# Delta stage: decayed keys and decayed state by scaled ACT copies in place of GpSimd products

## The reference, cut to what matters

```python
kd = k * jnp.exp(gc[..., -1:] - gc)[..., None]      # keys times the remaining decay
gl = jnp.exp(gc[..., -1])                           # decay over the whole chunk
def step(state, inp):
    u_n, w_n, qk_n, qg_n, kd_n, gl_n = inp
    v_new = u_n - jnp.einsum('bhtd,bhdv->bhtv', w_n, state)
    o = jnp.einsum('bhtd,bhdv->bhtv', qg_n, state) + jnp.einsum('bhts,bhsv->bhtv', qk_n, v_new)
    state = state * gl_n[..., None, None] + jnp.einsum('bhsd,bhsv->bhdv', kd_n, v_new)
    return state, o
```

## Time and profile before

| | us |
|---|---|
| median of 3 runs | 3032.19 |
| lowest, highest | 3027.72, 3032.43 |
| the profiled execution, its own time | 3031.88 |
| its span in the profile | 3029.9 |

### The profile page before, as it was taken

How to read it: one execution, slowest core, us unless ns; L and a number is a source line. 1 busy time by engine, 2 the same in 40 slices (tenths; PEclk the granted TensorE clock), 3 DMA queues, 4 the chain that set the end, 5 groups by cost and what they waited for, 6 DMA issues and landing times. The chain is left out here.

```text
span 3029.9 us, 42610 instructions
## 1 busy us (share of the span) xinstructions
PE 2863.9 (95%) x17750; PEld 2342.2 (77%) x17750; DVE 1450.3 (48%) x2014; ACT 1177.7 (39%) x1861; POOL 1001.0 (33%) x540
## 2 busy tenths in 40 slices
PE   6988998999999989989989999999889999999999
PEld 4788977878888757889768788887577767788887
DVE  4565556437616345655573375262584552441120
ACT  3563645323313235627552332221443652342232
POOL 2263021014534422630210244443442223344433
PEclk9999999999999999999999999999998999999999
DMA  5101202333423241022023333231522223333332
GB/s 161 34 28 60 80 1 71 94 101 91 116 79 103 58 112 54 5 69 70 2 71 104 104 91 111 82 103 45 122 77 60 70 61 87 86 97 98 92 89 77
DMA packets 419840, 235.92 MB, mean 78 GB/s; under 512 B 24020, under 2 KB 416706, under 8 KB 419010
## 3 DMA queue, kind: packets, MB, share of 16 engines
q1 hardware_dynamic: 419650, 233.20, 27.2%
HBM read 226.88 MB, written 6.29 MB: 77 GB/s over the span
## 5 line engine op out<-in xcount | busy, mean ns | idle before, releaser
L2066 POOL TENSOR_TENSOR WLO<-RAW,WHI 128x1024 fp32r<-128x1024 f32 (+1 forms) x205 | 534.3, 2611 | 982.7 <-ACT WHI L1947 982.7
L144 PE MATMUL PS<-HHI,WHI 128*128 128x512 f32 x2016 | 798.7, 396 | 24.7 <-POOL HLO L563 14.6
L145 PE MATMUL PS<-HLO,WHI 128*128 128x512 f32 x2016 | 790.5, 392 | 0.0
L146 PE MATMUL PS<-HHI,WLO 128*128 128x512 f32 x2016 | 790.4, 392 | 0.0
L144 PEld LDWEIGHTS PS<-HHI,WHI 128*128 128x128 f32 x2016 | 381.1, 189 | 118.1 <-POOL HLO L563 16.2
L145 PEld LDWEIGHTS PS<-HLO,WHI 128*128 128x128 f32 x2016 | 381.0, 189 | 83.1 <-issue 2.7
L146 PEld LDWEIGHTS PS<-HHI,WLO 128*128 128x128 f32 x2016 | 380.6, 189 | 82.5
L1947 ACT CAST WHI<-RAW 128x1024 fp32r<-128x1024 f32 (+1 forms) x208 | 227.4, 1099 | 550.0 <-PE PS L146 538.2
L2060 DVE TENSOR_TENSOR X<-X,PS 128x512 f32<-128x512 f32 x48 | 33.0, 688 | 372.4 <-PE PS L146 372.4
L144 PE MATMUL PS<-MHI,WHI 128*128 128x512 f32 x384 | 153.7, 400 | 16.0 <-DVE WLO L2019 11.1
L2043 DVE SCALAR_TENSOR_TENSOR ACC<-GP,PARS,ACC 128x512 f32<-128x512 f32 x88 | 162.8, 1850 | 3.1
(11 more groups left out here) (456 smaller groups left out, 5110.8 us busy)
## 6 DMA issues: line engine op xcount, KB each, us to landing
RAW<-in_w_up SPq DMA_DIRECT2D x88, 512.0 KB, 3.8
RAW<-in_w_in SPq DMA_DIRECT2D x82, 512.0 KB, 4.0
RAW<-in_w_mlp SPq DMA_DIRECT2D x64, 512.0 KB, 4.1
RAW<-in_w_down SPq DMA_DIRECT2D x32, 704.0 KB, 4.6
RAW<-in_w_in SPq DMA_DIRECT2D x20, 1024.0 KB, 5.4
RAW<-in_w_gate SPq DMA_DIRECT2D x32, 512.0 KB, 4.0
RAW<-in_w_out SPq DMA_DIRECT2D x24, 512.0 KB, 4.3
x_kept<-X SPq DMA_DIRECT2D x2, 2048.0 KB, 9.0
```

The lines of the kernel that those rows point to most:

```text
L144: e.matmul(out, wh, xh, start=first and n == 0, stop=False)
L145: e.matmul(out, wh, xl, start=False, stop=False)
L146: last = e.matmul(out, wl, xh, start=False, stop=final and n == len(quads) - 1)
L2066: pool.tensor_tensor(slot(WLO, u), source(u), slot(WHI, u), ALU.subtract).then_inc(lo_s, 1)
```

## The change

GpSimd's two functions go. ACT gets functions of the same names: for each lane four `activation(..., ACT.Copy, scale=...)`, one a head, whose scale is the column of LD or EL of that head, with the same semaphores at the end (`kd`, `sd`) and the same waits in front (`st` or `ld`, and `su`). In ACT's order, the keys of lane 0 stand ahead of `keep(2)`, those of lane 1 ahead of `keep(3)`, and the state of both lanes behind `keep(5)`.

```diff
@@ GpSimd
-                def keys_decayed(m, d):
-                    pool.wait_ge(S["st"][d], m) if m else pool.wait_ge(S["ld"][d], 2)
-                    c = chunk(m, d)
-                    pool.tensor_tensor(B[d]["KD"], tok(KTOK, c), wide(B[d]["LD"][:, c, :], P), ALU.mult).then_inc(S["kd"][d], 1)
-
-                def state_decayed(m, d):
-                    pool.wait_ge(S["su"][d], m)
-                    pool.tensor_tensor(B[d]["SD"], B[d]["ST"][:, :, :], wide(B[d]["EL"][:, chunk(m, d), :], P), ALU.mult).then_inc(S["sd"][d], 1)
...
                             level_mask(m, d, 5)
-                        if m and j < CH - 1:
-                            keys_decayed(j, d)
-                            if j:
-                                state_decayed(j, d)
@@ ACT
+                def keys_decayed(m, d):
+                    if m < CH - 1:
+                        if m:
+                            act.wait_ge(S["st"][d], m)
+                        else:
+                            act.wait_ge(S["ld"][d], 2)
+                        c = chunk(m, d)
+                        for h in H4:
+                            last = act.activation(B[d]["KD"][:, h, :], tok(KTOK, c)[:, h, :], ACT.Copy, scale=B[d]["LD"][:, c, h:h + 1])
+                        last.then_inc(S["kd"][d], 1)
+
+                def state_decayed(m, d):
+                    if 0 < m < CH - 1:
+                        act.wait_ge(S["su"][d], m)
+                        for h in H4:
+                            last = act.activation(B[d]["SD"][:, h, :], B[d]["ST"][:, h, :], ACT.Copy, scale=B[d]["EL"][:, chunk(m, d), h:h + 1])
+                        last.then_inc(S["sd"][d], 1)
...
                         for d in lanes:
                             keep_last(j, d)
+                        keys_decayed(j, 0)
                     keep(2)
                     if after:
                         for d in lanes:
                             grown(m + 1, d)
                         decays(m + 1, 0)
+                    if m:
+                        keys_decayed(j, 1)
                     keep(3)
...
                     keep(5)
+                    if m:
+                        for d in lanes:
+                            state_decayed(j, d)
                     if after:
                         for d in lanes:
                             corner_times_beta(m + 1, d)
```

## The result

| | before | after |
|---|---|---|
| median of 9 runs each, us | 3029.61 | 3044.95 |
| lowest, highest | 3026.85, 3039.07 | 3042.04, 3047.78 |
| the profiled execution, its own time | 3031.88 | 3043.67 |
| its span | 3029.9 | 3041.6 |
| mean granted clock of TensorE | 0.977 | 0.975 |

The ratio is 1.0048, 95% interval 1.0037 to 1.0058. By this ratio it is 14.5 us more (the two medians lie 15.3 us apart), slower beyond what the scatter explains. The forecast was 3036.5 us with a range of 3031.5 to 3040.5 and "same" as its likeliest side. It was wrong.

The account below looks back on a forecast made before the run. TensorE, busy 95% of the span, was taken to bound the kernel by its own order. Delays of 1.19 + 0.99 = 2.18 us a layer, 4.36 in two, on 3032.19 gave 3036.5 us, range 3031.5 to 3040.5.

Parts of the forecast that it names:

- The price of a group: Four added ACT copies of 128x128 in the delta stage take 1.19 us, between 1.01 and 1.56 us.
- The direct delay: Lane 1's keys ahead of keep(3) make TensorE's level_d 3 late by 1.19 us in m = 1, 0.99 in m = 2.
- Rival A: TensorE has more slack, or ACT's freed order absorbs the groups: no change, 3032 us; chance 0.11.
- The hidden groups: Lane 0's keys, lane 1's in m = 3 and the state copies fall in ACT's waits and cost nothing.
- GpSimd's relief: Twenty products leaving GpSimd free 20.7 us of its time, worth nothing on the path.
- Rival D: GpSimd's relief counts, removing three 0.59 us gaps a layer: 3033 us with the delay, 3028.7 without; chance 0.05.
- Rival C: The added ACT copies don't overlap, a group taking 1.56 us: 3038.0 us; chance 0.09.
- No fall of the clock behind the new gaps: TensorE's clock stays at 1.00 behind the gaps ahead of level_d 3, 1.47 us in m = 1, about 1.0 in m = 2.
- Rival B: TensorE's clock falls behind the new gaps, 1.26 us a fall: 3039.0 us for two, 3041.6 for four; chance 0.07.
- the sum: Delays of 1.19 and 0.99 us make 2.18 us a layer, 4.36 us in two, added to the time of before.
- So it moves along, and the next stage starts behind the last product: A late level_d 3 in the delta stage isn't given back; everything behind it shifts by the same delay.
- if the time moved by more outside these two stages: Sign of being wrong: time changing by more outside the two delta stages, one a layer, that the change touches.

Follow-up runs that it names:

- keys1_behind: Kernel after, with the keys of lane 1 moved behind keep(3) and the gates of lane 1 in ACT's order; 3030.85 us, ratio 1.0009 to before.
- idle_copies: Kernel before, GpSimd's products kept, plus four unread ACT copies ahead of keep(3) in m = 1 and 2 of both layers; 3042.49 us, ratio 1.0042.
- filled pair: Kernels after and before plus unread TensorE products in the idle times of hgrn_stage; 3030.1 us (0.9985) and 3029.84 us (0.9983).
- low_on_vector pair: Kernels before and after with the FL subtraction of hgrn_stage moved from GpSimd to VectorE; 3017.11 us (0.9950) and 3018.55 us (0.9955).

## Why the prediction was wrong, point by point

- **The price of a group: right.** 1.19 us forecast, 1.17 measured. By the formula that was quoted from the Trainium skill (ScalarE: Activation LUTs, What ACT_TABLE_LOAD costs) 1.17 was the estimate; the trace agrees with it.
- **The direct delay: right in place, a little too large.** Forecast gaps of 1.47 and about 1.0 us, measured 1.30 and 0.76 to 0.77. The forecast let L868 start where L881 had; it starts 0.11 to 0.13 us sooner behind the second EG copy (in m = 1 187.91 - 187.42 = 0.49 us behind that copy's start, where L881 had 188.84 - 188.22 = 0.62), which takes that much off both gaps; why it does was not tried. 3.6 us in place of 4.36, and the stages grew by 2.4 and 1.8 for a forecast of 2.2 each. Rival A, no change, falls by the gaps.
- **The hidden groups: right.** keep(2) has 0.42 us to spare (0.4 forecast); in m = 3 1.60 us is left; the state's copies and the copies to O hold up nothing. keys1_behind shows it in the time: 1.0009 with these groups in place.
- **GpSimd's relief is worth nothing: right, as far as the times tell** (keys1_behind, idle_copies). Rival D falls: the 0.59 us gaps are still there. Rival C, copies that don't overlap, falls by the 1.17 us.
- **No fall of the clock behind the new gaps: right,** at 1.30, 0.77 and (idle_copies) 1.45 us. Rival B had the right mechanism and the wrong place: it priced a fall only at the gap that the change makes, and at 1.26 us, where one in `hgrn_stage` cost about 1.6. That its sum for four falls, 3041.6 us, lies nearest to the measured time is luck.
- **The step that failed is the sum:** "So it moves along, and the next stage starts behind the last product", and then 4.36 us added to the time of before. That holds only if every later stage takes as long when it starts 2 us later; the term for the later stages stood at nothing, without a reason. It was not weighed, though the earlier trace rows showed the low clock in this kernel and though the prediction itself named "if the time moved by more outside these two stages" as a sign of being wrong. What the runs showed in its place: hgrn 2, which the change doesn't touch, is 4.6 us longer by three falls of the clock, and the 14.5 us come down to 0.3 when the idle times of `hgrn_stage` are filled and to 1.4 when they are shortened. In its level work TensorE waits seven times for VectorE's operands, up to 2.3 us at a time; in the profiled before, three falls lay in it in layer 1 and none in layer 2, at the same idle times. Whether the clock falls behind such a wait isn't set by the wait alone. A delay upstream goes with it: none in layer 2 in three traces without a delay, two or three in each of seven traces with one.

How much of 14.5 us this is: the base plays no part, since the 14.5 are a difference (the three runs of before that the forecast stood on had a median of 3032.19, the nine 3029.61). 3.6 us is the direct delay. Three falls in hgrn 2 are some 4.8 us. In layer 1 the four traces with a delay ahead in that layer have 2 or 3 falls and the six without have 0 (twice), 2 or 3 (four times), so anything from nothing to 4.8 us more in a median, which single traces can't pin down. The filled pair shows by the time itself that 14.2 of the 14.5 us go when these idle times are filled, and the low_on_vector pair that 13 go when they are shortened, in each case with part of the direct delay made up in other stages. These shares overlap, and no run separates them to the microsecond; that the idle times of `hgrn_stage` carry most of what goes beyond the 3.6 us is shown by those two pairs, and that they act through falls of the clock by the level-work table; the exact split is not shown.

What stays open: why a later start brings the falls in layer 2 each time, when the idle times ahead of them look the same, whether delays of other sizes than those run here (1.5 to 3.5 us in one layer, 3.6 in two) would bring them or take them away, and why the median of before itself moves between sets from 3027.0 to 3034.2 us: each set ran on another chip, and the median of the granted clock went with it (0.978, 0.976, 0.978, 0.977), but why the clock differs was not tried.

## What to carry to other kernels

A delay of a microsecond on the path does not only move what is behind it: ask which later stages have repeated idle times of TensorE of two microseconds, and put a few falls of the clock (1.6 us each here) with their chance into the range, on both sides. When a small edit costs several times its direct delay, compare the lengths of the stages that it doesn't touch, with their granted clock, before looking for a cause at the edit. Such a stage is better mended than steered around: its idle times were two-input VectorE products beside GpSimd, and moving one subtraction off GpSimd won 0.5% and took nearly all of the sensitivity away.

## What the runs showed of the hardware

- The granted clock of TensorE stayed at its upper level behind single idle times of 1.30 to 1.74 us and fell behind 3.78 and 3.95 us. In `hgrn_stage` it fell in some executions and stayed in others behind the same waits: 2.3 us, 2.2 us, 1.3 and 1.1 us close together, and 0.93 and 0.72 us at its start. A fall in its level work cost about 1.6 us.
- A VectorE product of 128x256 with both inputs in SBUF took 1.38 to 1.48 us beside a GpSimd subtraction and 0.41 or 0.42 us without it.
- The scaled ACT copy of the state (L930) has a median of 423 ns, that of the keys (L923) 388 ns, the same size and form; why was not tried.
